# Head 0's probabilities of group B turned by VectorE behind an SBUF-to-SBUF exchange, for steps 32 to 53

## What is computed

```python
def mixer_b(q, k, v, rel_table):
    ...
    logits = jnp.einsum('bcqhd,bckhd->bhcqk', qc, kb) * SCALE
    logits = logits + bias[:, None]
    logits = jnp.where(valid[:, None, :], logits, NEG)
    p = jax.nn.softmax(logits, axis=-1)
    out = jnp.einsum('bhcqk,bckhd->bcqhd', p, vb)
```

## Time and profile before

| | |
|---|---|
| median of 3 runs | 1033.53 us (1033.47 to 1033.95) |
| span of the profiled execution | 1031.9 us |
| TensorE busy | 1023.0 us, 99% |
| VectorE busy | 770.9 us, 75% |
| ScalarE busy | 470.5 us, 46% |
| GpSimd busy | 219.7 us, 21% |
| steps 32 to 53 in the span | 171 to 289 us |

### The profile page before, as it was taken

The page is one execution under the profiler, slowest core; times in us unless marked ns, Lnnn a source line. Parts: engine busy times, 40 slices in busy tenths (PEclk is TensorE's granted clock), DMA queues, the critical chain, the costliest instruction groups (busy, mean ns, idle before and its releaser), DMA issues.

```text
span 1031.9 us, 15795 instructions
## 1 busy us (share of the span) xinstructions
PE 1023.0 (99%) x5525; PEld 851.0 (82%) x5525; DVE 770.9 (75%) x1506; ACT 470.5 (46%) x978; POOL 219.7 (21%) x218
## 2 busy tenths in 40 slices
PE   9999999999999999999999999999999999999997
PEld 8899887788778888878888888888888888888886
DVE  4955677867688578888988788786444777778997
ACT  6632355545477567836221221311344445454562
POOL 5200000000000003148675674761100000000000
PEclk9999999999999999999999999999999999999999
DMA  9835442111071474045444434446777733454344
GB/s 202 222 98 136 108 134 77 42 47 37 11 225 43 123 188 159 21 143 212 171 167 155 163 134 152 163 144 225 243 243 242 229 103 92 143 194 142 93 142 164
DMA packets 135071, 147.92 MB, mean 143 GB/s; under 512 B 72248, under 2 KB 85440, under 8 KB 132944
## 3 DMA queue, kind: packets, MB, share of 16 engines
q1 hardware_dynamic: 133920, 146.68, 45.7%
q10 hardware_dynamic: 688, 0.20, 0.1%
q0 software_dynamic: 384, 0.04, 0.0%
HBM read 103.65 MB, written 47.49 MB: 146 GB/s over the span
## 4 chain that ended last, share of the span: by engine, by line
PE 94%; DVE 3%; issue 1%; DMA 1%; ACT 0%; POOL 0%; DVEq 0%; ACTq 0%; POOLq 0%
PE ps L2242 27%; PE ps L2244 27%; PE ps L2243 27%; PE ps L2451 3%; PE ps L2465 3%; PE ps L2432 2%; PE ps L2376 1%; DVE wc_lo L1918 1%; PE ps L2411 1%; PE ps L2584 1%; PE ps L2586 1%; PE ps L2572 1%; DMA up_raw<-in_w_up 1%; DVE b_lo L1907 1%; PE ps L2254 0%
## 5 line engine op out<-in xcount | busy, mean ns | idle before, releaser
L2242 PE MATMUL ps<-b_hi,wc_hi 128*128 128x512 f32 x448 | 174.6, 390 | 0.5 <-DVE wc_lo L1918 0.5
L2243 PE MATMUL ps<-tm_lo,sm_hi 128*128 128x512 f32 (+1 forms) x450 | 174.6, 388 | 0.0
L2244 PE MATMUL ps<-tm_hi,sm_lo 128*128 128x512 f32 (+1 forms) x450 | 174.6, 388 | 0.0
L2242 PE MATMUL ps<-tm_hi,sm_hi 128*128 128x512 f32 (+1 forms) x450 | 174.6, 388 | 0.0
L2244 PE MATMUL ps<-b_hi,wc_lo 128*128 128x512 f32 x448 | 174.3, 389 | 0.0
L2243 PE MATMUL ps<-b_lo,wc_hi 128*128 128x512 f32 x448 | 174.3, 389 | 0.0
L1485 ACT ACTIVATE sm_hi<-sm_raw 128x512 fp32r<-128x512 f32 x112 | 70.7, 631 | 161.8 <-DMA sm_raw<-u_matrices 161.8
L2146 DVE TENSOR_TENSOR sm_lo<-sm_raw,sm_hi 128x512 fp32r<-128x512 f32 x112 | 77.4, 691 | 77.9 <-ACT sm_hi L1485 77.3
L2242 PEld LDWEIGHTS ps<-b_hi,wc_hi 128*128 128x128 f32 x448 | 84.1, 188 | 18.3 <-DVE wc_lo L1918 0.9
L2242 PEld LDWEIGHTS ps<-tm_hi,sm_hi 128*128 128x128 f32 x450 | 84.5, 188 | 17.6
L2244 PEld LDWEIGHTS ps<-tm_hi,sm_lo 128*128 128x128 f32 x450 | 84.5, 188 | 17.4
(11 more groups left out here) (261 smaller groups left out, 2063.2 us busy)
## 6 DMA issues: line engine op xcount, KB each, us to landing
u_matrices<-stage SPq DMA_DIRECT2D x112, 256.0 KB, 2.0
sm_raw<-u_matrices SPq DMA_DIRECT2D x112, 256.0 KB, 2.6
up_raw<-in_w_up SPq DMA_DIRECT2D x16, 1024.0 KB, 5.0
w<-in_w_down SPq DMA_DIRECT2D x64, 256.0 KB, 3.8
w_raw<-in_w_in SPq DMA_DIRECT2D x8, 512.0 KB, 3.5
xr<-in_x SPq DMA_DIRECT2D x8, 512.0 KB, 4.3
x_rows<-xr SPq DMA_DIRECT2D x8, 512.0 KB, 4.1
xf<-x_rows SPq DMA_DIRECT2D x8, 512.0 KB, 3.5
```

The lines of the kernel that those rows point to most:

```text
L2242: pe.matmul(out, w_hi_, x_hi_, start=start, stop=False)
L2243: pe.matmul(out, w_hi_, x_lo_, start=False, stop=False)
L2244: return pe.matmul(out, w_lo_, x_hi_, start=False, stop=stop)
```

## The change

For steps 32 to 53 (`turned_b`) head 0 no longer goes over TensorE. ScalarE, not VectorE, multiplies its row block by the reciprocal, and writes it, with its columns regrouped by quarters of 32 keys, into slot 2 of `prob_b` (`sent_probs`). Head 0's scores and exponentials of all these steps use slot 0. SP then issues four DMAs from `prob_b` to a new buffer `turn_in` in SBUF, one per quarter: each takes 128 partitions to 32 partitions with four column groups. VectorE transposes `turn_in` in blocks of 32x32 straight into `probT_b` (`turn_probs`). Head 1 keeps its path: only its transposes and copies are left, in chunks of four tiles and one with five keys. In the weighing, head 0's queries come out as four groups of 32, and the matmul writes them to every fourth column of its PSUM block, which restores their order. The counts for the new waits use semaphores that exist: s_rowp (head 0 scaled by ScalarE), s_rcol (transposed by VectorE), s_tab (landed).

```diff
+def turned_b(n):
+    return A_STEPS <= n < LATE
...
-    if paired(n) and nk <= 2:
-        return [(0, 2 * nk, nk == 1)]
+    if turned_b(n):
+        return [(nk, nk, True)] if nk < B_KEYS else [(nk, 4, True), (nk + 4, 1, False)]
...
+            def exchange_step(n):
+
+                m = keys_of(n) * 32
+                sp.wait_ge(s_pb, pb0 + n - A_STEPS + 1)
+                if n == A_STEPS:
+                    sp.wait_ge(s_pv, A_STEPS)
+                else:
+                    sp.wait_ge(s_tb, tb0 + n - A_STEPS)
+                for a in range(4):
+                    sp.dma_start(turn_in[32 * a:32 * a + 32, 0:4 * m].rearrange("j (c m) -> j c m", c=4),
+                                 sent_probs(n)[:, a * m:a * m + m]).then_inc(s_pld, 16)
...
+            for n in range(A_STEPS, LATE):
+                exchange_step(n)
+                if n == A_STEPS:
+                    load_bias(5)
+                elif n % T == T - 1:
+                    sp.wait_ge(s_nm, 2 * n + 2)
+                    load_bias(n // T + 2)
+                elif n % 4 == 1 and n // 4 - 2 < FILL_TILES:
+                    load_fill(n // 4 - 2)
...
+            def normalize(n):
+
+                at = 2 * (n % 2)
+                act.wait_ge(s_ri, 2 * n + 1)
+                if n > A_STEPS:
+                    act.wait_ge(s_pld, pld0 + 64 * (n - A_STEPS))
+                nc.scalar.activation(quarters_first(sent_probs(n)), blocks_first(prob_of(n, 0)[:, first_column(n):]),
+                                     ACT.Copy, scale=rinv[0][:, at:at + 1]).then_inc(s_pb, 1)
...
                     if hh == 0:
                         dve.wait_ge(s_qk, n + 1)
+                        if A_STEPS < n <= LATE:
+                            dve.wait_ge(s_pb, pb0 + n - A_STEPS)
+                        elif n == LATE + 1:
+                            dve.wait_ge(s_pld, pld0 + 64 * (LATE - A_STEPS))
...
+            def turn_probs(n):
+
+                dve.wait_ge(s_pld, pld0 + 64 * (n - A_STEPS + 1))
+                dve.wait_ge(s_pv, n - 1)
+                cols = slice(0, keys_of(n) * P)
+                nc.vector.transpose(prob_t(n, 0)[:, cols], turn_in[:, cols]).then_inc(s_tb, 1)
...
-                if n < STEPS and not (paired(n) and n % 2):
+                if n < STEPS and not odd:
                     for hh in range(2):
                         normalize(n, hh)
-                if n < LATE and n != A_STEPS + 2 and not paired(n - 1):
+                if A_STEPS < n <= LATE:
+                    turn_probs(n - 1)
+                if paired(n) and not odd:
+                    scores(n + 1)
+                if n <= LATE:
                     copies_of(n - 1)
-                if paired(n) and n % T == 0:
-                    scores(n + 1)
-                if paired(n) and n % 2 == 0:
+                if paired(n) and not odd:
                     for hh in range(2):
                         normalize(n + 1, hh)
...
+                if turned_b(n):
+                    pe.wait_ge(s_tb, tb0 + n - A_STEPS + 1)
...
+                        out_ = ps[64 * hh:64 * hh + 64, 7, (t % 4) * P:(t % 4) * P + P]
+                        if hh == 0 and turned_b(n):
+                            out_ = out_.rearrange("p (j c) -> p c j", c=4)
```

More of the change, by code:

```diff
@@ L500, in chunk_copy @@
             out = ps[:, CHUNK_BANKS[n, c][0], 0:count * P]
-            if nk == B_KEYS:
+            if nk == B_KEYS and not turned_b(n):
                 return heads.rearrange("p h n -> p (h n)")[:, first * P:(first + count) * P], out
-            nh = count // nk
-            return heads[:, first // nk:first // nk + nh, 0:nk * P], out.rearrange("p (h n) -> p h n", h=nh)
+            return heads[:, first // nk, first % nk * P:(first % nk + count) * P], out
         def odd_values(t):
@@ L1247, in _ @@
             for n in range(A_STEPS, STEPS + 3):
+                odd = paired(n) and n % 2 == 1
                 if n == A_STEPS + 2:
@@ L1251, in _ @@
                     store_mix((n - 6) // 4)
-                if A_STEPS < n < LATE and not paired(n - 1):
+                if odd:
+                    normalize(n)
+                if A_STEPS < n <= LATE and not paired(n - 1):
                     copy_chunk(n - 1, 0)
@@ L1255, in _ @@
                     tiles_hi(halves_done(n - 1))
-                if n < STEPS and not (paired(n) and n % 2):
-                    for m in (n, n + 1) if paired(n) else (n,):
+                if n < STEPS and not odd:
+                    for hh in range(2):
+                        exp(n, hh)
+                    if turned_b(n):
+                        normalize(n)
+                    if paired(n):
                         for hh in range(2):
-                            exp(m, hh)
+                            exp(n + 1, hh)
                 if n == A_STEPS:
@@ L1262, in _ @@
                     store_first_mix(n)
-                if paired(n) and n % 2:
+                if odd:
                     for m in (n - 1, n):
[L1265 to L1268, removed]
+                        copy_chunk(m, 0)
+                if LATE < n <= STEPS:
+                    for c in range(len(chunks_of(n - 1))):
                         if chunks_of(n - 1)[c][2]:
                             copy_chunk(n - 1, c)
-                    if n != LATE:
-                        tiles_hi(halves_done(n - 1))
+                if n <= STEPS and n != LATE:
+                    tiles_hi(halves_done(n - 1))
                 splits(n)
@@ L2513, in _ @@
                 if paired(n) and n % 2:
-                    for c in range(len(chunks_of(n - 1))):
-                        transposes(n - 1, c)
+                    transposes(n - 1, 0)
                     if n % T == 1:
@@ L2518, in _ @@
                 elif not paired(n - 1):
-                    transposes(n - 1, 0)
-                    transposes(n - 1, 1)
+                    for c in range(len(chunks_of(n - 1))):
+                        transposes(n - 1, c)
                 for m in range(first, end):
@@ L2523, in _ @@
                         transposes(n, 0)
-                        transposes(n, 1)
-                    elif m == first + 2 and len(chunks_of(n - 1)) == 3:
-                        transposes(n - 1, 2)
                     fill(m)
-                if first + 2 >= end and len(chunks_of(n - 1)) == 3:
-                    transposes(n - 1, 2)
                 if n >= LATE:
```

77 lines of the change are left out of this document (42 added, 35 removed).

## The result

| | before | after |
|---|---|---|
| median of the runs, us | 1033.57 (1033.47 to 1033.95) | 1041.68 (1039.34 to 1042.54) |
| the profiled execution, us | 1033.5 | 1041.9 |
| its span, us | 1031.9 | 1040.1 |
| TensorE busy in it, us | 1023.0 | 1020.9 |

The change costs 8.1 us; the ratio of the runs is 1.0075, with an interval of 1.0061 to 1.0089. The forecast was 1036.0 with a range of 1031 to 1046: the sign came out and so did the mechanism (a serial relay whose waits cost more than the removed transposes give), and the size did not, since 2.6 us were forecast. 1041.7 also lies outside the 1033 to 1039 that the prediction gave to this mechanism alone.

The account below looks back on a forecast made before the run. TensorE's own instructions were taken to bound the kernel, the other engines keeping up. Net of removed transposes and new waits, +1.5 - 0.2 + 0.3 + 1.0 = +2.6 us on 1033.53 gave 1036.0, range 1031 to 1046.

Parts of the forecast that it names:

- rival 2: Head 0's weighing: the strided PSUM write is slow, about 0.12 us more per matmul, 1045, up to 1053; chance 0.25.
- What is removed, 8.4 us: TensorE, steps 32 to 53: head 0's 80 transposes go, at 0.105 us each.
- Length of an exchange, 4.3: SP's four DMAs, from release to VectorE's start: 4.3 us, with 4.6 as upper end.
- Rival 3: Exchanges take 4.9 us or more because 512 descriptors crowd the queue; 1040; chance 0.1.
- VectorE's transpose, 0.84 and 0.3: VectorE's transpose of head 0 in the relay: 0.84 us for 640 columns, 0.3 for 128.
- Steps 32 to 39, +1.5: Start of the relay, few keys: 3.6 us waited against 2.1 removed, so 1.5 us slower.
- Steps 40 to 47, -0.2: These steps, walked in detail: 2.95 us waited against 3.15 removed, so 0.2 us faster.
- Steps 48 to 53, +0.3: These steps, taken like steps 40 to 47 without their good end: 0.3 us slower.
- The end, +1.0: Steps 53 to 56: no fills left to cover VectorE's last transpose and a copy; 1.0 us slower.
- Elsewhere nothing: Output and fill weights are issued about 4 us later but still arrive in time; no cost.
- The strided output, zero: Head 0's weighing writes every fourth PSUM column; taken as costing zero, upper bound 18.7 us.
- About 9 us of waits from 171 to 290: TensorE's waits on other engines between 171 and 290 us of the trace would total about 9 us.

Follow-up runs that it names:

- fewer_t: Kernel before, most of head 0's TensorE transposes in steps 32 to 53 left out with nothing in their place (output wrong); 1027.88 us, ratio 0.9942.
- copy_tail: Changed kernel, at step 54 alone VectorE's copy of step 53's fifth head-1 tile put ahead of the transpose of 53; 1038.70 us.
- strided_write: Kernel before, head 0's weighing of steps 32 to 53 writing every fourth PSUM column, probabilities read in plain order; 1033.60 us, ratio 0.9996.
- one_quarter: Changed kernel, only the first of each exchange's four DMAs kept in steps 37 to 53 (output wrong); 1033.03 us, ratio 0.9990.
- order2: Changed kernel, VectorE's copy ahead of the transpose at even steps, transpose between the two reciprocals at steps 37, 39, 45, 47, 53; 1035.27 us.
- second_pair: Kernel before, with the relay in steps 44 to 47 alone and VectorE's order as in order2; 1033.31 us, ratio 0.9993.
- two_queues: Changed kernel, third and fourth DMA of each exchange in steps 33 to 53 issued by ScalarE instead of SP; 1049.93 us, ratio 1.0152.

## Why the prediction was right in kind and short in size

That 1041.7 lies inside 1031 to 1046 is in part luck. The upper end stood there for rival 2, a slow PSUM write, which did not occur; the prediction's own mechanism had been given 1033 to 1039. Term by term:

- **What is removed, 8.4 us:** right within a tenth. 0.095 us each by fewer_t against 0.105, so about 7.6.
- **Length of an exchange, 4.3:** right for the quiet ones (4.2 with five keys at steps 45 and 47, 3.8 with one or two), short for the long ones: 4.9 at step 37, 4.8 at 39, 5.4 at 40, 4.9 at 53. The landing was taken as one number, 2.1 from the last issue; it measured 1.9 to 3.5. The upper bound of 4.6 came from one exchange and was too low. Rival 3 (4.9 or more, 1040) had the nearer time, but by crowding of its own descriptors; the quiet exchanges, which move the same, took 4.2.
- **VectorE's transpose, 0.84 and 0.3:** right to the digit (0.84, 0.30).
- **Steps 32 to 39, +1.5:** right in sum (+1.8), by luck in its parts. The fill of 34 didn't wait (0.5 forecast), the weighing of 33 waited 0.64 (1.3), the transposes of 35 0.87 (0.6), their weighing 0.58 (0.8), and the weighing of 37 waited 1.03, where 0.4 around step 38 had been forecast.
- **Steps 40 to 47, -0.2:** the first step that failed, by 2.2 us (by 1.2 in copy_tail, the same program there). The walk let step 39's weighing wait 0.25; it waited 1.65. Its exchange was issued when the walk said (4.5 after the scores' end) but landed 0.5 later, and the copy that the weighing also needs stood behind the transpose and behind the scores of step 41, 1.0 more. The walk followed the transpose as what the weighing waits for and forgot the copy, which it had named itself. The waits of 0.4 before a fill and 0.6 before the transposes of 41 came out as 0.17 and none, that before the transposes of 43 as 0.88 instead of 0.2.
- **Steps 48 to 53, +0.3:** right (+0.2).
- **The end, +1.0:** the second step that failed, by 3.3. Exchange 53 landed at 298.8, after step 54's first transposes at 297.7, with a fetch in it and no fill to cover it. That costs 2.3, and as much in copy_tail, where it landed 2.30 after its last issue; the other 2.0 are the clock. No step of the prediction asked what a wait of 1.6 us does to TensorE's clock.
- **Elsewhere nothing:** right, though the output weights went out at 296.5 and not at 293.
- **The strided output, zero:** right (strided_write), against rival 2, which had been given 0.25.
- **About 9 us of waits from 171 to 290:** right, 8.7 are listed. But up to step 54 TensorE lost 11.8 us (3.9 late, with 75 transposes or 7.9 us less to do). A wait costs more than the row says: from step 44's scores to 45's it takes 6.50 us instead of 5.71, 0.79 more, where the row lists 0.57. The listed wait begins at the end of the matmul before, which in an unbroken stream overlaps the next one. By 0.22 us each, the 13 waits up to 290 us make about the missing 3 us, an estimate from this one place. The walk reckoned a wait at its bare length.

So the theory of the serial relay stands: one_quarter shows the length, order2 the place in VectorE's order, and they are two ends of the same waits, since a turn is exchange plus transpose. What stays open is what makes some exchanges long, and how often the clock falls: the four runs of the changed kernel spread over 3.2 us, the four of the kernel before over 0.5 (the 21 beside second_pair over 2.6).

## What to carry to other kernels

A relay over single buffers has no slack to share: count the whole turn from buffer free to buffer free, with the place of each part in its engine's order, and keep at least a microsecond over the quiet landing, since 1.9 to 2.3 us became up to 3.5 here. Look for every operand that the waiting instruction needs and not only for the new one. Don't put a wait for another engine, nor the issues behind it, into the stream of a busy one (two_queues). Moving the new instruction into a gap that the engine already waits in, together with the earlier copies (order2), brought back three quarters of the loss, the clock's share among it.

## What was not expected of the hardware

- With the moving operand of head 0 read at one float in four, the 40 weighing records of both heads took 4.79 us instead of 2.40; a PSUM output at the same pattern is free (31.2 us for 480 with and without).
- The last of an exchange's four DMAs is issued 1.9 us behind the first whether they carry 16 or 80 KB each, and it lands 1.9 to 2.3 us later, or 3.0 to 3.5 in 13 of 14 exchanges with a 16 KB instruction fetch near it (2.47 in the other).
- Around a wait of 1.63 us the granted clock fell to 0.50 for 6.8 us; around one of 2.00 at the same place in another kernel it stayed at 1.00. Around the wait before weighing 39 it was the other way round: no fall at 1.65, and one of 3.4 us at 1.96.
